# A hybrid diffusion step with two expert layers: one gate product moved into the router, and the first expert pair reordered

## The reference

```python
for l in range(DEPTH):
    mp = adaln(cond_ctx, ada_w[l], ada_b[l])          # silu(cond) @ w + b, six vectors of 1024
    ms = adaln(c, ada_w[l], ada_b[l])
    hp = modulate(xp, norm_mix[l], mp[0], mp[1])      # RMS norm, times (1 + scale), plus shift
    hs = modulate(xs, norm_mix[l], ms[0], ms[1])
    ...                                               # op, os_ = the layer's mixer of hp and hs
    xp = xp + mp[2] * op                              # mp[2], ms[2]: the mixer's gate
    xs = xs + ms[2] * os_
    hp = modulate(xp, norm_ffn[l], mp[3], mp[4])
    hs = modulate(xs, norm_ffn[l], ms[3], ms[4])
    xp = xp + mp[5] * hier_moe(hp, ...)
    xs = xs + ms[5] * hier_moe(hs, ...)

def hier_moe(h, wg, bg, we, be, w1, w3, w2):
    ...                                               # best group of 4, then its best 2 of 4 experts
    h1 = jnp.einsum('nd,edf->nef', x, w1)
    h3 = jnp.einsum('nd,edf->nef', x, w3)
    a = jax.nn.silu(h1) * h3 * comb[:, :, None]
    return jnp.einsum('nef,efd->nd', a, w2).reshape(B, T, D)
```

## Time and profile before

| | |
|---|---|
| median of three runs | 796.29 us (793.76 to 797.00) |
| the profiled execution's own time | 796.88 us |
| its span | 795.1 us |
| TensorE busy | 767.8 us, 97% of the span |
| VectorE, ScalarE busy | 342.3 us, 176.4 us |
| moved by the DMA queues | 277.13 MB, mean 349 GB/s |
| mean granted TensorE clock | 0.995 |

### The profile page before, as it was taken

How to read it: one execution, slowest core, us unless ns; L and a number is a source line. 1 busy time by engine, 2 the same in 40 slices (tenths; PEclk the granted TensorE clock), 3 DMA queues, 4 the chain that set the end, 5 groups by cost and what they waited for, 6 DMA issues and landing times.

```text
span 795.1 us, 10222 instructions
## 1 busy us (share of the span) xinstructions
PE 767.8 (97%) x3993; PEld 379.3 (48%) x3993; DVE 342.3 (43%) x783; ACT 176.4 (22%) x433; POOL 2.2 (0%) x9
## 2 busy tenths in 40 slices
PE   7999999999899999999999899999899999999997
PEld 2364535545544444344334657645544444344334
DVE  2226188225831642544327312325822643445326
ACT  4111565205421101101113401205311101110111
POOL 0000000000000000000000000000000000000000
PEclk9999999999999999999999999999999999999999
DMA  8969999933599999999999992024599999999995
GB/s 347 426 213 429 428 429 426 419 142 127 209 366 419 422 421 421 421 420 422 421 415 423 428 399 108 1 106 173 198 374 411 421 420 422 421 420 421 421 419 213
DMA packets 41779, 277.13 MB, mean 349 GB/s; under 512 B 8781, under 2 KB 9825, under 8 KB 13825
## 3 DMA queue, kind: packets, MB, share of 16 engines
q1 hardware_dynamic: 41233, 275.03, 84.5%
q10 hardware_dynamic: 432, 1.28, 0.4%
q0 software_dynamic: 64, 0.13, 0.0%
HBM read 274.72 MB, written 1.70 MB: 348 GB/s over the span
## 4 chain that ended last, share of the span: by engine, by line
PE 83%; DMA 7%; DVE 4%; ACT 2%; SPq 1%; issue 1%; DVEq 1%; ACTq 0%
PE bank L1982 25%; PE bank L2007 12%; PE bank L1873 10%; PE bank L1967 6%; PE bank L1812 5%; PE bank L2409 5%; PE bank L2013 4%; DMA ring<-in_ada_w 4%; PE bank L2271 4%; DMA ring<-in_moe_w 3%; PE bank L2233 3%; SPq L890 1%; PE bank L2323 1%; PE bank L2344 1%; PE bank L1837 1%
## 5 line engine op out<-in xcount | busy, mean ns | idle before, releaser
L1982 PE MATMUL bank<-ring,Z 128*64 128x512 f32 x1024 | 226.5, 594 | 0.6 <-DMA ring<-in_moe_w 0.6
L1982 PEld LDWEIGHTS bank<-ring,Z 128*64 128x64 f32 x1024 | 72.5, 137 | 137.5 <-issue 135.4
L2007 PE MATMUL bank<-ring,Z 128*64 128x512 f32 (+1 forms) x544 | 113.9, 570 | 0.8 <-DMA ring<-in_moe_w 0.8
L1873 PE MATMUL bank<-ring,T 128*128 128x512 f32 x192 | 83.1, 592 | 0.0
L2007 PEld LDWEIGHTS bank<-ring,Z 128*64 128x64 f32 x544 | 38.0, 137 | 68.6 <-issue 66.8
L1485 DVE TENSOR_TENSOR Z<-Z,bank 128x512 f32<-128x512 f32 x16 | 11.0, 687 | 127.0 <-PE bank L1982 127.0
L1873 PEld LDWEIGHTS bank<-ring,T 128*128 128x128 f32 x192 | 36.2, 190 | 44.0 <-issue 44.0
L1812 PE MATMUL bank<-ring,cond 128*32 128x512 f32 x384 | 48.4, 627 | 5.4 <-DMA ring<-in_ada_w 5.2
L2013 PE MATMUL bank<-ys,Cs 128*128 128x512 f32 (+1 forms) x204 | 52.3, 391 | 1.1 <-DVE ys L1502 1.1
L1515 DVE TENSOR_TENSOR x<-x,bank 128x512 f32<-128x512 f32 x84 | 52.1, 680 | 0.3
L1151 ACT ACTIVATE ys<-wg 128x512 fp32r<-128x512 f32 (+1 forms) x34 | 20.6, 606 | 136.1 <-DVE wg L1497 136.1
(11 more groups left out here) (243 smaller groups left out, 742.4 us busy)
## 6 DMA issues: line engine op xcount, KB each, us to landing
ring<-in_moe_w SPq DMA_DIRECT2D x184, 1024.0 KB, 15.6
ring<-in_ada_w SPq DMA_DIRECT2D x23, 2048.0 KB, 17.8
ring<-in_moe_w SPq DMA_DIRECT2D x16, 512.0 KB, 20.7
ring<-in_a_w_out SPq DMA_DIRECT2D x2, 2048.0 KB, 16.5
ring<-in_f_w_in SPq DMA_DIRECT2D x2, 2048.0 KB, 30.7
ring<-in_f_w_out SPq DMA_DIRECT2D x2, 2048.0 KB, 31.3
ring<-in_ada_w SPq DMA_DIRECT2D x2, 1024.0 KB, 7.8
ring<-in_a_w_in SPq DMA_DIRECT2D x4, 512.0 KB, 19.0
```

The costliest lines, as they stand in the source:

```text
L1873: last = pe.matmul(b[:, :], T[:, k, i * P:(i + 1) * P], w[:, k, :], start=(k == 0), stop=(k == KT - 1))
L1982: last = pe.matmul(out[BLK * u:BLK * (u + 1), :], xT[:, b, k, s0 + BLK * u:s0 + BLK * (u + 1)], w[:, k, :], start=(k == 0), stop=(k == KT ...
L2007: last = pe.matmul(out, aT[:, k, BLK * u:BLK * (u + 1)], down_columns(w2, k, a, e), start=(k == 0), stop=(k == FC - 1), skip_group_check=True)
```

## The change

There are two parts.

1. The product of piece 20 moves from behind `moe(0)` into layer 0's router, in the place of that layer's second `busy(3)`. Its weights move in the list of items from behind the 48 expert blocks to ahead of them. Its high part (ScalarE) and low part (VectorE) move into the router too; its row stays in SBUF until `ada_read(20)`, which stays where it was. In the plan the product takes bank 7, and behind `moe(0)` only piece 21 is left, now ahead of the normalised tokens. The wait for `back_out` between the two products goes.
2. In pair 0 of both layers the first halves of w3 are multiplied right behind the first halves of w1, ahead of gather steps 2 and 3; SP loads the first halves of blocks 7 to 10 ahead of their second halves; and gather step 5 is split in two, one half ahead of `middle` and one behind it.

```diff
@@ plan()
+        if l == 0:
+            t.fill(("ada", 20), "dve", bank=7)
         of_gather[l] = [t.of[t.last[bank]][2:4] for bank in (2, 3)]
         for h in range(2):
             t.empty(("tokens", l, 2, h))
+        if l == 0:
+            t.empty(("ada", 20))
...
-    for n in (20, 21):
-        t.fill(("ada", n), "dve")
-    norm(2, 0, 1, step=t.fill)
...
+    t.fill(("ada", 21), "dve")
+    norm(2, 0, 1, 2, step=t.fill)
+    for i in range(NT):
         for q in range(2):
             t.empty(("norm", 2, i, q))
+        if i == 0:
+            t.empty(("ada", 21))
@@ the list of items
-    before0 = ... + halves(a_w_out) + ada_items[18:20]
-    before1 = ada_items[20:22] + halves(f_w_in) + ...
+    before0 = ... + halves(a_w_out) + ada_items[18:21]
+    before1 = ada_items[21:22] + halves(f_w_in) + ...
@@ SP
-                for j in range(NS, 6 * (NPAIR - 1), 2):
+                blocks_in_turn(*range(NS, NS + 4))
+                for j in range(NS + 4, 6 * (NPAIR - 1), 2):
@@ ACT, between the layers, and at the end of the router
                     affine(2, 0)
-                    ada_product(20)
+                    ada_product(21)
                     affine(2, 1)
-                    ada_product(21)
...
                 ada_read(n + 1)
+                if l == 0:
+                    ada_product(20)
@@ DVE, router, and between the layers
                 low_part(l, NT - 1)
+                if l == 0:
+                    gate_parts(20)
...
             affine(2, 0)
-            gate_parts(20)
+            gate_parts(21)
             affine(2, 1)
-            gate_parts(21)
@@ PE, end of the router
                 ada_read(n + 1)
-                busy(3)
+                if l == 0:
+                    ada_product(20)
+                else:
+                    busy(3)
@@ PE, pair 0
                         up_part(out, 0, s0, weights(0), 2, 4).then_inc(s["up_half"], 1)
+                        arrive(2, 0)
+                        up_part(psH, 0, s0, weights(2), 0, 4).then_inc(s["up_half"], 1)
                         gather_step(2)
                         gather_step(3)
...
+                    if first:
+                        gather_half(4 * (q + 1) + 1, 0)
                     pe.wait_ge(s["prod_out"], p + 1)
                     middle(s)
                     if first:
-                        gather_step(4 * (q + 1) + 2 * half + 1)
+                        gather_half(4 * (q + 1) + 1, 1)
@@ PE, behind moe(0)
-            ada_product(20)
-
-            pe.wait_ge(pairs[0]["back_out"], (NPAIR - 1) * 2 * NT + NT + 1)
             ada_product(21)
             norm(2, 0, 1, 2)
```

More of the change, by code:

```diff
@@ L456, in build @@
     halves = lambda w: [w[0], w[1]]
-    before0 = ada_items[0:1] + w_in_items[0:1] + ada_items[1:4] + w_in_items[1:] + ada_items[4:18] + halves(a_w_out) + ada_items[18:20]
-    before1 = ada_items[20:22] + halves(f_w_in) + halves(f_w_out) + ada_items[22:24]
+    before0 = ada_items[0:1] + w_in_items[0:1] + ada_items[1:4] + w_in_items[1:] + ada_items[4:18] + halves(a_w_out) + ada_items[18:21]
+    before1 = ada_items[21:22] + halves(f_w_in) + halves(f_w_out) + ada_items[22:24]
     N_EXP0 = len(before0)
@@ L464, in build @@
     N_WOUT = 4 + 3 + 14
-    N_FIN = N_MIX1 + 2
+    N_FIN = N_MIX1 + 1
     N_FOUT = N_FIN + 2
@@ L470, in ada_at @@
         start = 0
-        for end, at in ((1, 0), (4, 2), (18, 4 + 3), (20, N_WOUT + 2), (22, N_MIX1), (24, N_FOUT + 2)):
+        for end, at in ((1, 0), (4, 2), (18, 4 + 3), (21, N_WOUT + 2), (22, N_MIX1), (24, N_FOUT + 2)):
             if n < end:
@@ L1959, in first_gather, with gather @@
                     last.then_inc(s["gathered"], 1)
-                def gather(s, out, k0, k1, w):
+                def gather(out, k0, k1, w):
                     for k in range(k0, k1):
@@ L1968, in gather, with gather_half @@
                                                  start=(t == 0 and part == 0), stop=(t == NT - 1 and part == 1))
-                    last.then_inc(s["gathered"], 1)
-                def gather_step(n):
+                    return last
+                def gather_half(n, i):
                     q, step = n // 4, n % 4
@@ L1976, in gather_step @@
                         pe.wait_ge(s["x_cols"], n - 1)
-                    gather(s, psX[step % 2], 2 * step, 2 * step + 2, QUAD)
+                    last = gather(psX[step % 2][:, i * QUAD:(i + 1) * QUAD], 2 * step + i, 2 * step + i + 1, QUAD)
+                    if i:
+                        last.then_inc(s["gathered"], 1)
+                def gather_step(n):
+                    for i in range(2):
+                        gather_half(n, i)
                 def up_part(out, b, s0, ws, k0, k1):
@@ L2060, in up @@
                     def up(out, k):
-                        arrive(k, 0)
-                        up_part(out, q % 2, s0, weights(k), 0, KT // 2).then_inc(s["up_half"], 1)
+                        if not first:
+                            arrive(k, 0)
+                            up_part(out, q % 2, s0, weights(k), 0, KT // 2).then_inc(s["up_half"], 1)
                         if last and k == 2:
@@ L2176, in moe @@
                             pe.wait_ge(o["sel_ready"], j * NT + NT)
-                            gather(o, psX[0], 0, KT, BLK)
+                            gather(psX[0], 0, KT, BLK).then_inc(o["gathered"], 1)
                             pe.wait_ge(o["x_cols"], j + 1)
```

## The result

| | before | after |
|---|---|---|
| median | 796.33 us (20 executions, 793.76 to 799.84) | 791.90 us (20 executions, 788.65 to 794.73) |
| profiled execution, own time | 796.88 us | 790.44 us |
| its span | 795.1 us | 788.6 us |

The ratio is 0.9948, with a 95% interval of 0.9937 to 0.9959: 4.2 us less by the ratio, 4.4 by the medians, with 3.3 to 5.0 us as bounds. So the kernel is faster. The median gain is just past the 0.5% (4.0 us) that the prediction called telling, and the interval reaches to both sides of it. The prediction had said 790.3, within 788.0 to 793.3. The two profiled executions lie 6.4 us apart, and the forecast of 6.6 was worked out from the one of before.

The account below looks back on a forecast made before the run. TensorE bounds the expert pairs, with loads slightly slower and living on the ring's lead; behind layer 0's experts a gate piece holds TensorE. Gains of 0.65, 0.05, 4.95 and 0.95 sum to 6.6: 796.9 to 790.3 us, range 788.0 to 793.3.

Parts of the forecast that it names:

- Behind layer 0's experts: Between layer 0's experts and uT: piece 21's product is hidden, VectorE sets uT, which starts at 441.85, not 446.81; gain 4.95 us.
- The router and the slots: Layer 0's router and the ring's slots: piece 20's product and transfer fit into waits and idle queue; cost 0.
- Rival 3: Block 6 goes out with first refills (router product after about 213), stream 5 us later; 795 us; 0.13 with lesser losses.
- The first pair: Pair 0 of both layers: half the gather step fills the wait ahead of middle; down starts 0.65 us earlier per layer.
- The refills: Loads in pair 0: stream 0.65 us earlier by TensorE, 0.3 by fuller queue; worth 0.05 in layer 0, 0.95 in layer 1.
- The clock: TensorE ahead of uT: clock expected to hold over the transposes; a fall costs 0.8 to 1.7 us, twice up to 2.4.
- Rival 1: The clock falls ahead of uT, among the transposes behind layer 0's experts; 791.1 to 792.7 us; chance 0.24.
- the forecast's own range: Whole kernel: 789.4 to 791.3 us around the forecast of 790.3; chance 0.48.
- The sum: Whole kernel: 0.65 + 0.05 + 4.95 + 0.95 = 6.6 us off 796.9, giving 790.3 us.

Follow-up runs that it names:

- first part alone: The kernel before with piece 20's weights and product in the router, piece 21 alone behind layer 0's experts, pair 0 as before: 792.51 us, ratio 0.9959.
- both pieces early: The changed kernel with piece 21 moved like piece 20: weights ahead of the experts, product in layer 0's router: 793.72 us, ratio 0.9965 against the kernel before.
- second part alone: The kernel before with first halves of w3 ahead, loads of blocks 7 to 10 by first halves, gather step 5 in two: 794.33 us, ratio 0.9985.
- the wrong order of loads: The changed kernel with TensorE's new order, but loads of blocks 7 to 10 two by two as before: 797.94 us, ratio 1.0018 against the kernel before.

## Why the prediction was right, and where its sizes were off

*Behind layer 0's experts.* Right in each step: piece 21 lands where piece 20 did (221.0 against 221.1 us with the first part alone), its product is hidden, and VectorE's three steps set `uT`. Forecast 8.0 us behind the start of piece 21's product (441.85 less 433.85), measured 7.83 (441.76 less 433.93). The size is right for the one traced execution (12.9 - 7.8 = 5.1 us) and too large for the times: the first part alone is worth 3.3 us (2.2 to 4.4). The term was read from a single execution. In the two other traces of before the same place has 11.6 us, 3.9 above 7.8, since the experts ended later there; and in all three the half rate doubled the product that I removed from the path, 1.6 us of the term. I had treated the fall as a danger to the changed kernel and not as a part of the base.

*The router and the slots.* Cost 0 forecast, 0 measured. Rival 3's condition did not arise: the product was over at 210.0, 3.5 us ahead of pair 0. With both pieces early it was over at 211.8, 3.0 us ahead of it, which is still not "later than about 213"; there the refills came 2.4 us late and the queue had no gap, so most of the lateness was made up. What block 6 behind the first refills would cost no run shows.

*The first pair.* 0.65 us a layer forecast, 0.67 measured at the place in layer 0. How much reaches the end the times do not show. In layer 1, the stretch from pair 0's start to the end of the kernel takes 225.6 to 226.9 us in six traces with the old code there and 224.9 to 226.7 in five with the new. The means are 0.6 us apart, where 0.95 was forecast, and the same code differs by more than that from execution to execution.

*The refills.* The step that failed: "blocks 11 and 12 take the slots of w2 ..., by which time the earlier refills are nearly through in either order". A gap in the refills of pair 0 is not closed by the later ones, because from then on the queue is full to the end of the layer (share 1.01 from 240 to 400 us). The gap was also sought in the wrong place: of the 2.2 idle us between 215 and 220, 1.15 lie ahead of the first refill, which no order of the refills can fill. What came back was the 0.9 us between 220 and 230 (share 0.91 before, 1.00 after). The second part alone moved piece 21's landing by some 2 us where 0.95 was forecast, and the wrong order of loads cost 6 us. For the changed kernel's time this error was small: on top of the first part the refills came 0.8 to 1.1 us earlier (221.0 us without, 219.9 and 220.2 with), about the 0.95 of the forecast. That this number fits is luck, since the step behind it is wrong.

*The clock.* Rival 1 is not seen in either trace of the changed kernel: the granted clock stayed at 1.00 over transposes with 1.5 us of gaps ahead of and between them. The rule in the Trainium skill (TensorE: Matmul & The Clock Gate, Part 4: PE-mode transpose), by which transposes don't count as a busy array, would have had it fall here; neither trace bears that out. The kernel with both pieces early speaks against it more plainly. There TensorE stood idle for 2.98 us and the clock fell; then it ran nothing but transposes from 439.55 to 443.89, and within them, near 443.3, the clock rose from 0.50 to 1.00. Still, the measured 791.9 lies where rival 1 had put the number (791.1 to 792.7) and outside the forecast's own range (789.4 to 791.3). The other executions were not traced, so a fall in some of them is not excluded; 11 of the 20 had a mean granted clock under 0.999, which the fall in the first 13 us can give too.

*The sum.* The two profiled executions say 6.4 us (796.88 against 790.44), the medians 4.4; the forecast was 6.6 for the first and 6.0 for the second. By place, the three traces of before and the two of the changed kernel differ in their means by 5.2 us from the start of pair 0 to `uT` (5.65 forecast), by nothing from there to layer 1's pairs (121.7 us in all five), and by 1.6 us in layer 1's pairs (0.95 forecast). So the traces bear out the forecast and the times only two thirds of it. Shown: all three traces of before had the fall, worth 1.6 us in each. Not shown: how often the fall comes (the weak estimate above takes 1 us off the 6.4), and the rest. Both traces of the changed kernel lie under its medians (by 1.5 and 2.7 us), the three of before 0.3 to 1.3 above; waits for blocks of up to 1.8 us a layer and the landing of the first weights vary from execution to execution, and I did not separate them. That the total came inside the range owes something to the range's width, 5.3 us.

## What to carry to other kernels

When TensorE and the loads take nearly the same time, a gap in the queue is paid for at the end of the phase, far from its cause: here 4.4 idle us at the start came back as 3.5 us of waits more than 160 us later. So look at the DMA share where the phase begins, not where the wait is, and compare stretches at the same distance from the phase's start. Move a load that stands behind such a phase to an idle stretch ahead of it, and with it the product that it feeds. A trace is one execution: if a stall in it sits beside a fallen clock, take the fall out of the base before you cost its removal, or take more than one trace.

## What the runs showed of the hardware that was not expected

- The granted clock fell to 0.50 after 2.07 us of waiting in one trace of the kernel before (439.83) and not after 1.84 us in the kernel with the second part alone (437.78), and over 24 transposes, which then took 4.51 us, behind an idle 2.98 us, in the kernel with both pieces early; with 0.90, 0.31 and 0.30 us ahead of groups of transposes it did not.
- With nothing but those 24 transposes running, the granted clock came back from 0.50 to 1.00 near 443.3.
- The order in which four 1 MB loads a layer were issued, with the same products and the same bytes, changed the whole kernel by some 6 us (797.94 against 791.90, on two chips; 5.6 by the ratios).
